# Two transformer blocks on one core: weight blocks and activation rows at a fixed distance modulo 256 bytes

## The reference, cut to what matters

```python
def first_block(...):
    h = h + hybrid_mixer(rms_norm(h, attn_norm_g[layer]), w_in[layer], ...)
    h = h + conv_ffn(rms_norm(h, ffn_norm_g[layer]), w_up[layer], ..., w_down[layer], valid)
    return rms_norm(h, final_norm_g)[:, PREFIX:]

def swiglu(x, w_gate, w_up, w_down):
    return (jax.nn.silu(x @ w_gate) * (x @ w_up)) @ w_down

def second_block(...):
    for l in range(DEPTH_2):
        h = h + 0.5 * swiglu(rmsnorm(h, ffn1_norm[l]), ffn1_w_gate[l], ffn1_w_up[l], ffn1_w_down[l])
        h = h + hybrid_mixer_2(rmsnorm(h, mix_norm[l]), w_in[l], ..., w_out[l])
        h = h + 0.5 * swiglu(rmsnorm(h, ffn2_norm[l]), ffn2_w_gate[l], ffn2_w_up[l], ffn2_w_down[l])
    return rmsnorm(h, final_norm)[:, N_META:]
```

## Time and profile before

| | us |
|---|---|
| median of 3 runs | 1459.07 (1458.87 to 1459.16) |
| the profiled execution's own time | 1458.79 |
| its span | 1457.0 |

### The profile page before, as it was taken

The page is one execution under the profiler, slowest core; times in us unless marked ns, Lnnn a source line. Parts: engine busy times, 40 slices in busy tenths (PEclk is TensorE's granted clock), DMA queues, the critical chain, the costliest instruction groups (busy, mean ns, idle before and its releaser), DMA issues.

```text
span 1457.0 us, 30945 instructions
## 1 busy us (share of the span) xinstructions
PE 1449.5 (99%) x11473; PEld 1417.6 (97%) x11473; DVE 903.2 (62%) x1576; ACT 770.0 (53%) x1113; POOL 493.6 (34%) x213
## 2 busy tenths in 40 slices
PE   9999999999999999999999999999999999999998
PEld 8899999889999999999999999999999999999987
DVE  6438888756446469988644434444447898864533
ACT  6546555555444446567544544444444657654443
POOL 6550000534334303710333432433420570044342
PEclk9999999999999999999999999999999999999999
DMA  7435666645556445455555654655644635567763
GB/s 269 131 113 162 177 185 203 210 149 173 173 173 213 163 131 165 143 156 166 175 175 173 203 180 129 185 172 182 201 151 145 174 119 186 174 195 202 208 189 114
DMA packets 74634, 250.92 MB, mean 172 GB/s; under 512 B 15808, under 2 KB 16704, under 8 KB 74560
## 3 DMA queue, kind: packets, MB, share of 16 engines
q1 hardware_dynamic: 74272, 249.38, 55.5%
q10 hardware_dynamic: 288, 0.54, 0.1%
HBM read 247.79 MB, written 1.05 MB: 171 GB/s over the span
## 4 chain that ended last, share of the span: by engine, by line
PE 98%; DVE 1%; ACT 0%; issue 0%; DVEq 0%; ACTq 0%
PE W L1697 27%; PE W L1698 27%; PE W L1699 27%; PE W L1785 3%; PE XP L1849 2%; PE XQ L1849 2%; PE W L1784 1%; PE W L1749 1%; PE W L1800 1%; PE W L1799 1%; PE W L1750 1%; PE W L1798 1%; PE W L1751 1%; PE XQ L1962 0%; PE XP L1854 0%
## 5 line engine op out<-in xcount | busy, mean ns | idle before, releaser
L463 POOL TENSOR_TENSOR wlo<-raw,whi 128x1024 fp32r<-128x1024 f32 (+1 forms) x185 | 473.1, 2562 | 913.0 <-ACT whi L538 912.6
L1697 PE MATMUL W<-xh,whi 128*128 128x272 f32 (+2 forms) x2400 | 689.6, 287 | 0.0
L1698 PE MATMUL W<-xl,whi 128*128 128x272 f32 (+2 forms) x2400 | 687.5, 286 | 0.0
L1699 PE MATMUL W<-xh,wlo 128*128 128x272 f32 (+2 forms) x2400 | 685.8, 286 | 0.0
L538 ACT ACTIVATE whi<-raw 128x1024 fp32r<-128x1024 f32 (+1 forms) x440 | 480.6, 1098 | 109.7 <-PE W L1699 68.2
L1697 PEld LDWEIGHTS W<-xh,whi 128*128 128x128 f32 x2400 | 452.4, 189 | 2.2 <-issue 1.2
L1699 PEld LDWEIGHTS W<-xh,wlo 128*128 128x128 f32 x2400 | 452.3, 188 | 0.0
L1698 PEld LDWEIGHTS W<-xl,whi 128*128 128x128 f32 x2400 | 451.1, 188 | 0.2
L1023 DVE TENSOR_TENSOR wlo<-raw,whi 128x1024 fp32r<-128x1024 f32 (+1 forms) x255 | 331.8, 1302 | 80.3 <-ACT whi L538 80.0
L1697 PE MATMUL W<-ax,whi 128*128 128x272 f32 (+2 forms) x816 | 234.5, 287 | 0.4 <-DVE ax L1467 0.3
L1699 PE MATMUL W<-ax,wlo 128*128 128x272 f32 (+2 forms) x816 | 234.3, 287 | 0.0
(11 more groups left out here) (293 smaller groups left out, 1401.0 us busy)
## 6 DMA issues: line engine op xcount, KB each, us to landing
raw<-in_w SPq DMA_DIRECT2D x377, 512.0 KB, 3.7
raw<-in_w SPq DMA_DIRECT2D x64, 704.0 KB, 4.1
proj<-proj SPq DMA_DIRECT2D x16, 64.0 KB, 3.8
scr<-in_cst SPq DMA_DIRECT2D x1, 1000.0 KB, 8.3
h<-in_hT SPq DMA_DIRECT2D x3, 272.0 KB, 4.4
raw<-in_w SPq DMA_DIRECT2D x2, 256.0 KB, 3.8
proj<-in_gain SPq DMA_DIRECT2D x1, 512.0 KB, 5.0
out<-proj SPq DMA_DIRECT2D x4, 128.0 KB, 1.8
```

What stands on the lines that cost most here:

```text
L463: pool.tensor_tensor(wlo[:, j, 0:cols], raw[:, j, 0:cols], whi[:, j, 0:cols].bitcast(F32), ALU.subtract).then_inc(lo_ready[j], 1)
L1697: pe.matmul(out, whi[:, j, w], mh, start=start and k == 0, stop=False, skip_group_check=True)
L1698: pe.matmul(out, whi[:, j, w], ml, start=False, stop=False, skip_group_check=True)
L1699: ins = pe.matmul(out, wlo[:, j, w], mh, start=False, stop=stop and k == len(rhs) - 1, skip_group_check=True)
```

## The change

It moves data in SBUF; the products that are summed are the same.

- Slots of `whi` and `wlo` get 1440 floats instead of 1408, so that an odd slot starts 32 floats off modulo 64. `raw` stays packed. Inside a slot the blocks are spaced: the step from block to block is that of the moving rows modulo 64 floats (144 for x, 160 for the mixers' outputs, 128 in the down product, 544 for 512-wide blocks of the last product), and the first block starts at a place that `column` works out, so that the moving row starts `behind` floats behind the weights modulo 64: -16 in most cases, -26 for rows that start at token 14, 0 in two cases of 256-token rows.
- `ax` becomes two planes, all high parts and then all low parts, with rows of 288 floats instead of 272.
- The down product takes even chunks in its first slab and odd ones in its second; the weights are arranged so before the launch.
- Rounding and subtracting read `raw` packed and write the spaced blocks, as accesses of 8 (11, 2) rows.
- `cst` keeps ones and identity. The sign tables and the mask go by a second DMA to rows RG to RG+3 of `proj`; `cst_landed` is waited for at 32, and VectorE waits for `minus_ready` before it writes row RG (slab 20).
- `keep_last` is allocated ahead of the slots. Some loops on GpSimd are written out.

```diff
+LINE, PITCH = 64, S11 + 32
+WHI_AT, WLO_AT, X_AT, ROW = 0, 0, 0, T + 16
+Place = namedtuple("Place", "blocks width step hi lo")
+X_BEHIND = {0: -16, T_A: -26, T_B: -16}
+ACT_BEHIND = {0: (-16, -16), T_A: (-26, -26), T_B: (-16, -16)}
+DOWN_BEHIND = {0: (-16, -16), T_B: (0, -16)}
+TOKEN_BEHIND = (0, 0)
+def column(moving, weights, j, behind):
+    return (moving - weights - LINE // 2 * (j % 2) - behind) % LINE
+def x_place(t, j):
+    return Place(DC, P, P + T % LINE, column(X_AT + t, WHI_AT, j, X_BEHIND[t]), column(X_AT + t, WLO_AT, j, X_BEHIND[t]))
+def a_places(t):
+    high, low = ACT_BEHIND[t]
+    return tuple(Place(DC, P, P + ROW % LINE, column(X_AT + t, WHI_AT, j, high), column(X_AT + t, WLO_AT, j, low))
+                 for j in range(4))
+def d_places(t):
+    high, low = DOWN_BEHIND[t]
+    return tuple(Place(HALF, P, P, column(X_AT + t + j % 2 * ROW, WHI_AT, j, high),
+                       column(X_AT + t + j % 2 * ROW, WLO_AT, j, low)) for j in range(4))
...
+        keep_last = sb("keep_last", [P, 2, T - 2 * P], F32R)
         raw = sb("raw", [P, 4, S11])
-        whi = sb("whi", [P, 4, S11], F32R)
-        wlo = sb("wlo", [P, 4, S11], F32R)
+        whi = sb("whi", [P, 4, PITCH], F32R)
+        wlo = sb("wlo", [P, 4, PITCH], F32R)
...
-        ax = sb("ax", [P, FC, 2, T], F32R)
-        ah, al = ax[:, :, 0, :], ax[:, :, 1, :]
+        ax = sb("ax", [P, 2, FC, ROW], F32R)
+        ah, al = ax[:, 0, :, 0:T], ax[:, 1, :, 0:T]
...
+        signs = proj[:, RG:RG + 4, :].rearrange("p c t -> p (c t)")[:, 0:2 * P + SBW]
...
+        def packed(j, place, a=0, e=None):
+            e = place.blocks if e is None else e
+            return raw[:, j, place.width * a:place.width * e].rearrange("p (k n) -> p k n", n=place.width)
+        def spread(weights, at, j, place, a=0, e=None):
+            e = place.blocks if e is None else e
+            return weights[:, j, at + place.step * a:at + place.step * e].rearrange(
+                "p (k n) -> p k n", n=place.step)[:, :, 0:place.width]
...
-            sp.dma_start(cst[:, :], cst_d).then_inc(cst_landed, 16)
+            sp.dma_start(cst[:, :], cst_d[:, 0:2 * P]).then_inc(cst_landed, 16)
+            sp.dma_start(signs, cst_d[:, 2 * P:]).then_inc(cst_landed, 16)
...
-                pool.tensor_tensor(wlo[:, j, 0:cols], raw[:, j, 0:cols], whi[:, j, 0:cols].bitcast(F32),
+                pool.tensor_tensor(low(j, place), packed(j, place), high(j, place).bitcast(F32),
                                    ALU.subtract).then_inc(lo_ready[j], 1)
...
-                act.activation(whi[:, j, 0:cols], raw[:, j, 0:cols], ACT.Copy).then_inc(hi_ready[j], 1)
+                act.activation(high(j, place), packed(j, place), ACT.Copy).then_inc(hi_ready[j], 1)
...
+                    if s == RG:
+                        dve.wait_ge(minus_ready, 1)
...
+                    wh, wl = weights(j, places[j], at + k)
+                    pe.matmul(out, wh, mh, start=start and k == 0, stop=False, skip_group_check=True)
+                    pe.matmul(out, wh, ml, start=False, stop=False, skip_group_check=True)
+                    ins = pe.matmul(out, wl, mh, start=False, stop=stop and k == len(pairs) - 1,
...
-                    c = half * HALF + k
+                    c = 2 * k + half
...
 def down_slabs(w):
-    return [tiles(w[half * HALF * P:(half + 1) * HALF * P], c) for c in chunk_cols(0, DC) for half in range(2)]
+    rows = w.reshape(FC, P, D)
+    return [tiles(rows[half::2].reshape(HALF * P, D), c) for c in chunk_cols(0, DC) for half in range(2)]
```

More of the change, by code:

```diff
@@ L21 @@
+from collections import namedtuple
 from contextlib import ExitStack
@@ L57, with x_places, t_places @@
 S11 = HALF * P
+LINE, PITCH = 64, S11 + 32
[9 more added lines that the diff above has]
+    return Place(DC, P, P + T % LINE, column(X_AT + t, WHI_AT, j, X_BEHIND[t]), column(X_AT + t, WLO_AT, j, X_BEHIND[t]))
+def x_places(t, up=None):
+    return tuple(x_place(up if up is not None and j % 2 else t, j) for j in range(4))
+def a_places(t):
[6 more added lines that the diff above has]
+                       column(X_AT + t + j % 2 * ROW, WLO_AT, j, low)) for j in range(4))
+def t_places():
+    high, low = TOKEN_BEHIND
+    return tuple(Place(2, HALF_D, HALF_D + ROW % LINE, (X_AT + T_B + high - WHI_AT - LINE // 2 * (j % 2)) % LINE,
+                       (X_AT + T_B + low - WLO_AT - LINE // 2 * (j % 2)) % LINE) for j in range(4))
 BLK = [(0, 128), (128, 256), (256, 272)]
@@ L483, in _ @@
             pool.tensor_tensor(wffr[:, 1, :], wff, wffr[:, 0, :].bitcast(F32), ALU.subtract).then_inc(gate_step, 1)
[L484 to L487, removed]
+            for s in range(2, 6):
+                slab_lo(s)
             pool.wait_ge(ff_step, 2)
-            lo(1, 2, S8)
-            pool.wait_ge(cst_landed, 16)
+            slab_lo(6)
+            pool.wait_ge(cst_landed, 32)
             pool.tensor_copy(identr[:, :], ident).then_inc(hide_ready, 1)
@@ L537, in hi @@
                     act.wait_ge(mm_done, 4 * g + j - 3)
-                act.activation(whi[:, j, 0:cols], raw[:, j, 0:cols], ACT.Copy).then_inc(hi_ready[j], 1)
+                act.activation(high(j, place), packed(j, place), ACT.Copy).then_inc(hi_ready[j], 1)
             def hi_ahead(g, j, own, nxt):
-                dg, slot, cols, _ = ahead(j, own, nxt)
-                hi(g + dg, slot, cols, first=isinstance(g, int) and g + dg == 0)
+                dg, slot, place, _ = ahead(j, own, nxt)
+                hi(g + dg, slot, place, first=isinstance(g, int) and g + dg == 0)
             def sqrt_stat(p, t=0, fin=False):
@@ L705, in _ @@
             hi_part(1, 1)
-            hi(0, 2, S8, first=True)
+            hi(0, 2, first_x(2)[2], first=True)
             act.wait_ge(mm_done, 1)
@@ L1728, in stat, with project @@
                 pe.matmul(X[3][:, t:T], ones, acc[:, t:], start=True, stop=True, skip_group_check=True).then_inc(stat_mm, 1)
-            def project(g, j, rhs, each=None, behind=3, t=0, between=None):
+            def project(g, j, rhs, behind=3, t=0):
                 emptied(4 * g + j - behind)
-                slab(g, j, rhs, W[j][:, t:T], each=each, between=between).then_inc(mm_done, 1)
+                slab(g, j, rhs, W[j][:, t:T]).then_inc(mm_done, 1)
             STAT_AT = 5
@@ L1836, in group @@
                             continue
-                        slab(g + i, j, a_rhs(t)[half * HALF:(half + 1) * HALF], W[j - half][:, t:T], start=half == 0,
-                             stop=half == 1, each=(al_ready, FC * f + half * HALF, 0) if first and j < 2 else None).then_inc(mm_done, 1)
+                        slab(g + i, j, d_rhs(half), W[j - half][:, t:T], start=half == 0, stop=half == 1,
+                             each=(al_ready, FC * f + half, 2) if first and j < 2 else None).then_inc(mm_done, 1)
                 group(0, first=True)
```

310 lines of the change are left out of this document (170 added, 140 removed).

## The result

The changed kernel takes 1447.77 us (median of four runs, 1447.57 to 1447.96), the kernel before 1459.01 us beside it: the ratio is 0.9923, with a 95% interval of 0.9911 to 0.9936. It is 11.2 us faster. The forecast was 1432 us, 27 us faster, with a range of 1405 to 1461: the sign and the place of the gain were right, its size was less than half.

The account below looks back on a forecast made before the run. TensorE's work bounds the kernel: the number of matmuls times the distance between their starts. Five terms sum to 27.3 us off the profiled 1458.8; with 0.3 added the forecast was 1432 us, range 1405 to 1461.

Parts of the forecast that it names:

- Placement counts: All matmuls: the place of moving rows relative to weights modulo 256 bytes matters, by some 5 ns a matmul.
- Part 1, the terms: Weight blocks and rows: rows fixed 16 floats before the weights make matmuls cheaper, 27.3 us in sum.
- Down products: 1584 matmuls of 272 columns go from 125.6 to 122.5 ns, gaining 4.9 us.
- Projections of 272 columns: 4464 matmuls over xh and xl go from 126.1 to 122.8 ns, gaining 14.7 us.
- Projections of 256 and 258 columns: 2736 matmuls gain 2.0 ns each, from 118.4 to 116.4 ns, 5.5 us.
- The rest over ax: 864 matmuls in the mixers' outputs, 256 to 272 columns, gain 1.5 ns each, 1.3 us.
- The pairs: 176 pairs of 256 and 512 columns gain 5 ns a pair, 0.9 us.
- Parts 2 to 4: Rounding and subtracting into spaced blocks, the new down chunk order and tables in two DMAs: no cost.
- No change (1459): Placement shifts time between matmuls but not their sum, so the time stays 1459 us; chance 0.10.
- The full gain (1400): The fixed relation frees the moving rows altogether, 59 us gained, 1400 us; chance 0.14.
- Rival 3: A constant distance holds every matmul in a dear relation, at 128.3 ns with 272 columns, 1482 us; chance 0.06.
- ScalarE (1479): ScalarE's rounding into 8 spaced rows takes 2445 ns each and delays the mixers, 1479 us; chance 0.06.

Follow-up runs that it names:

- e4_packed: The changed kernel with all weight blocks packed again at multiples of 256 bytes, planes, tables and chunk order kept; 1459.32 us, ratio 1.0002 to the kernel before.
- e2_one_column: The changed kernel with reads held on one column in three 272-column feed-forward projections: weights', moving rows', then both; 1432.19 us.
- e7_x24: The changed kernel with weights of all 272-column projections starting 24 floats after the moving row instead of 16; 1451.96 us, ratio 0.995.
- e12_again: The same kernel as e10_packed_parts, run once more; 1446.64 us, ratio 0.9915 to the kernel before.
- e10_packed_parts: The changed kernel with blocks packed again in the last product, the first block's up projections and the 256-column mixer outputs; 1446.41 us, ratio 0.9914.
- e6_short_rows: The changed kernel with the moving read repeating 16, 68 or 4 floats, one length for each of three 272-column projections; 1446.12 us.
- e9_uniform: The changed kernel with other row-to-weights distances, the same for all slots of a stage (such as 0, 32 or 30 floats); 1457.3 us.
- e5_scan: The changed kernel with row-to-weights distances set per slot and stage, a second table of them; 1454.41 us.

## Why the prediction was right in sign and wrong in size

**What bounds the kernel.** Right: the gain came from the pitch of matmuls and nothing else; TensorE's waits are 3.0 us, 2.0 before.

**Placement counts.** Right, and shown: with the blocks packed again the gain is gone (e4_packed). The rule of the Trainium skill ("TensorE: Matmul & The Clock Gate", section "Part 2: What happens when you issue a matmul") that the weights' load takes nothing from the running matmul, by which the time would have stayed at 1459, does not hold to that degree: 126.1 or 124.3 ns by the place of the weights alone. For the other 9 of the 12 ns, which go when the moving read stands still (e2_one_column), it is neither borne out nor refuted, since no run leaves the load out.

**Part 1, the terms.** This is the step that failed: "Within an odd chunk the second matmul ... takes 0.12 us; I read it as 122.5 ns", and all matmuls put in that relation were given that price. As a reading it was right: in the three down products of before, the 264 second matmuls of odd chunks take 122.4 ns in the mean. But the third ones right behind them take 126.6, and with every matmul in that relation the price was 123.55. A gap between two starts, even one that comes back in every chunk, holds what its neighbours left behind; e7_x24 shows it too, 122.96 ns for a slot among others and 125.0 for a stage of the same. The other basis was rounded: from chunks of 0.37, 0.38 and 0.39 us I read 123.3 and 128.3 ns, 5 apart, where the trace has 124.2 for odd and 127.0 for even chunks, 2.8 apart. Term by term:
- Down products: 4.9 us forecast; 1584 x (125.6 - 123.55) = 3.2 us measured, so 2.0 ns instead of 3.1.
- Projections of 272 columns: 14.7 us forecast; 7.5 us measured. In the three feed-forward stages it was 126.1 to 124.3, 1.8 ns instead of 3.3. The mean of two at 122.5 and one at 123.3 ns never came about. This term alone is 7 of the 16 us missed.
- Projections of 256 and 258 columns: 5.5 us forecast, 0.8 measured. 256 columns gained 1.4 us in the last stage, and e12_again shows that this much can also be lost from one execution to the next; 258 columns became dearer, 119.1 to 119.8 ns, and the 256 between them no cheaper: 237.5 ns for one of each before, 238.3 after, 236.9 and 237.5 packed (e10_packed_parts, e12_again). The 115.0 of the earlier trace rows was a stretch of ten matmuls right behind other ones, and no price either.
- The rest over ax: 1.3 us forecast, 0.3 measured.
- The pairs: 0.9 us forecast, 2.4 ns a pair and 0.4 us measured. The last product was left at nothing and cost 0.8 us more; packed again it cost nothing (e10_packed_parts).

**Parts 2 to 4.** Right, all at nothing. ScalarE's rounding into 8 spaced rows takes what it took in the earlier trace rows, and VectorE's subtraction 1249 ns:

```profile
L618 ACT ACTIVATE whi<-raw 128x1024 fp32r<-128x1024 f32 x376 | 393.2, 1052 | 89.3 <-PE W L1797 49.2 <-PE W L1903 16.8 <-PE XP L1903 9.1
...
L1111 DVE TENSOR_TENSOR wlo<-raw,whi 128x1024 fp32r<-128x1024 f32 x223 | 278.4, 1249 | 59.4 <-ACT whi L618 59.1
```

In the mixer's window VectorE and ScalarE are busy 123.8 and 90.5 of 141 us, as in the earlier trace rows, while TensorE does 1151 matmuls instead of 1142 in it. No wait for a down chunk or for a table is in the list of waits; the last table is copied at 30.81 us, 0.38 later than in the earlier trace rows:

```profile
30.81 0.51 POOL L583 CAST minus_r<-proj 128x128 fp32r<-128x128 f32 x1
```

**The rivals.** No change (1459) was refuted by the ratio. The full gain (1400) was refuted, and a reason with it: most of the excess needs a moving read that walks (e2_one_column), and walking within 64 bytes is enough (e6_short_rows). Rival 3, being held in a dear relation, did not happen in the change, but its mechanism is real: e9_uniform holds whole stages at 126.58 ns, above the 126.1 and 125.6 of before, and takes 1457.3 us. I had put 0.06 on it because "nothing ties the cheap relation to its neighbours"; just that tie exists, it only cost gain and not loss. ScalarE (1479) was refuted by its 1052 ns.

## What to carry to other kernels

A pitch read from one place in a repeating pattern, or from ten matmuls right behind another kind, is no price: read the mean of a stage that holds one relation throughout, and where there is none in the trace, hope for less and keep the range wide. Before spending work on placement, hold one of the two reads still (one column, broadcast) in a stage: that shows in one run which of them the excess hangs on. Here 9 of the 12 ns hung on the moving read's walk, and the placement of the weights won 1.8 to 2.0. Apply a placement stage by stage, since spaced blocks gained 1.8 ns with 272 columns, lost 0.7 with 258, and lost 1.3% in the product of 512.

## What the runs showed of the hardware that I had not expected

- A matmul of 272 columns whose moving read stays within 16 bytes starts 115.8 ns after the one before; one that walks over 64 bytes or more takes 123.5 to 127.8 in the median of a stage, at every distance tried. At the granted clock of 1.00 the columns alone are 113.3.
- The weights' places modulo 256 bytes shift this by up to 3 ns in a whole stage: 123.55 or 126.58 in a down product, for distances of 16 and 32 floats.
- With 272 columns and distance 16 in the whole stage, the median slab agrees between profiles to 0.05 ns; a slot at 16 among others goes to and fro between 123.5 and 126.6 (e5_scan). The stage of 256 columns has two levels, 116.7 and 118.3 ns, taken by different executions of one kernel, 1.4 us apart in a time of 1447.
- What the weights' read does to the moving one (a shared bank, an arbiter, the order of two requests) no run here tells, and none shows the moving read without a load beside it.
